# Seven block products for the u, gate_c and xb projections of the mixer, with the convolution's taps on ScalarE and GpSimd

## The reference

```python
z = h @ w_in                                   # h is rmsnorm(x, mix_norm)
za, zb, zg = jnp.split(z, [2 * A_WIDTH, 2 * A_WIDTH + 3 * B_WIDTH], axis=-1)
u, v = jnp.split(jax.nn.gelu(za), 2, axis=-1)
y_a = spatial_gating(u, v, sgu_norm, sgu_w, sgu_b) @ w_proj_a
gate_b, gate_c, xb = jnp.split(zb, 3, axis=-1)
y_b = (gate_b * short_conv(gate_c * xb, conv_w)) @ w_proj_b
g_a, g_b = jnp.split(zg, 2, axis=-1)
merged = jax.nn.sigmoid(g_a) * y_a + jax.nn.sigmoid(g_b) * y_b
return merged @ w_out
```

## Time and profile before

| | us |
|---|---|
| median of 3 runs | 1713.25 (1713.06 to 1713.26) |
| the profiled execution, whole | 1713.5 |
| its span in the trace | 1711.8 |
| TensorE busy (matmul) | 1690.5, 99% |
| VectorE, ScalarE, GpSimd busy | 947.4, 736.7, 758.2 |
| the twelve units that change | 953.2 to 1083.9 |
| the gate_b units behind them | 1083.9 to 1134.7 |

### The profile page before, as it was taken

One profiled execution on the slowest core, in us unless ns is written; L12 is line 12 of the kernel. 1 busy time (PEld: TensorE's weight loads), 2 busy tenths in 40 slices (PEclk: granted clock), 3 DMA queues, 4 the chain that ended last, 5 costly groups with the idle time before them and its releaser, 6 DMA issues.

```text
span 1711.8 us, 25456 instructions
## 1 busy us (share of the span) xinstructions
PE 1690.5 (99%) x9725; PEld 1445.4 (84%) x9725; DVE 947.4 (55%) x1313; ACT 736.7 (43%) x1027; POOL 758.2 (44%) x366
## 2 busy tenths in 40 slices
PE   7999999999999999999999999999999999999998
PEld 4677788777788899998889888888888889999887
DVE  4645765665766777877220634641112587777412
ACT  4444773644573544445333322332222454445323
POOL 1342635233225454555444544344444445554552
PEclk9999999999999999999999999999999999999999
DMA  9614215112112223322323222222222222232222
GB/s 362 240 52 171 75 50 221 50 74 99 50 50 98 99 99 111 110 90 85 102 101 114 102 94 98 99 85 92 96 95 99 99 99 99 98 114 83 97 89 83
DMA packets 35061, 180.88 MB, mean 106 GB/s; under 512 B 4486, under 2 KB 6668, under 8 KB 19372
## 3 DMA queue, kind: packets, MB, share of 16 engines
q1 hardware_dynamic: 30876, 166.09, 27.1%
q10 hardware_dynamic: 4112, 13.80, 2.1%
HBM read 177.78 MB, written 2.10 MB: 105 GB/s over the span
## 4 chain that ended last, share of the span: by engine, by line
PE 89%; issue 4%; POOL 3%; SPq 1%; DVE 1%; DMA 1%; ACT 1%; POOLq 0%; DVEq 0%; ACTq 0%
PE ps L1354 22%; PE ps L1356 21%; PE ps L1355 21%; PE ps L1656 4%; PE ps L1658 3%; PE ps L1657 3%; POOL wl_both L659 3%; PE ps L1416 2%; PE ps L1421 2%; PE ps L1417 2%; PE ps L1723 1%; PE ps L1697 1%; SPq L566 1%; DMA ada_w<-w_ada 1%; PE ps L1710 1%
## 5 line engine op out<-in xcount | busy, mean ns | idle before, releaser
L659 POOL TENSOR_TENSOR wl_both<-raw_both,wh_both 128x1024 fp32r<-128x1024 f32 (+1 forms) x184 | 425.2, 2331 | 509.8 <-ACT wh_both L794 505.7
L1354 PE MATMUL ps<-xh,wh_both 128*128 128x512 f32 (+1 forms) x880 | 315.2, 358 | 1.2 <-POOL wl_both L681 1.2
L1356 PE MATMUL ps<-xh,wl_both 128*128 128x512 f32 (+1 forms) x880 | 312.1, 355 | 0.0
L1355 PE MATMUL ps<-xl,wh_both 128*128 128x512 f32 (+1 forms) x880 | 312.0, 355 | 0.0
L794 ACT ACTIVATE wh_both<-raw_both 128x2048 fp32r<-128x2048 f32 x91 | 174.2, 1915 | 317.4 <-PE ps L1356 306.0
L681 POOL TENSOR_TENSOR wl_both<-raw_both,wh_both 128x1024 fp32r<-128x1024 f32 x46 | 114.2, 2498 | 206.8 <-ACT wh_both L948 137.9
L1354 PEld LDWEIGHTS ps<-xh,wh_both 128*128 128x128 f32 x880 | 166.4, 189 | 31.5 <-issue 7.5
L1356 PEld LDWEIGHTS ps<-xh,wl_both 128*128 128x128 f32 x880 | 166.4, 189 | 23.6
L1355 PEld LDWEIGHTS ps<-xl,wh_both 128*128 128x128 f32 x880 | 166.5, 189 | 22.3
L703 POOL TENSOR_TENSOR wl_both<-raw_both,wh_both 128x1024 fp32r<-128x1024 f32 x72 | 131.9, 1854 | 105.7 <-DVE ps L2593 105.7
L1354 PE MATMUL ps<-fh,wh_both 128*128 128x512 f32 (+1 forms) x374 | 141.4, 378 | 1.0 <-issue 1.0
(11 more groups left out here) (362 smaller groups left out, 3990.2 us busy)
## 6 DMA issues: line engine op xcount, KB each, us to landing
raw_both<-ffn_in_stream SPq DMA_DIRECT2D x44, 1024.0 KB, 4.8
raw_both<-mixer_stream SPq DMA_DIRECT2D x40, 1024.0 KB, 4.8
raw_both<-layer_stream SPq DMA_DIRECT2D x36, 1024.0 KB, 5.9
raw_both<-ffn_out_stream SPq DMA_DIRECT2D x32, 704.0 KB, 4.1
ada_w<-w_ada SPq DMA_DIRECT2D x16, 512.0 KB, 11.3
ada_late<-w_ada ACTq DMA_DIRECT2D x16, 512.0 KB, 4.9
gate_w<-w_ada ACTq DMA_DIRECT2D x4, 1024.0 KB, 13.2
next_w<-w_ada SPq DMA_DIRECT2D x7, 512.0 KB, 8.9
```

The costliest lines, as they stand in the source:

```text
L659: last = nc.gpsimd.tensor_tensor(wl[u][:, cols], raw[u][:, cols], wh[u][:, cols].bitcast(F32), ALU.subtract)
L1354: nc.tensor.matmul(bank_ap, w0, x0, start=first, stop=False, skip_group_check=goes_on)
L1355: nc.tensor.matmul(bank_ap, w0, x1, start=False, stop=False, skip_group_check=goes_on)
L1356: return nc.tensor.matmul(bank_ap, w1, x0, start=False, stop=last, skip_group_check=goes_on)
```

## The change

Twelve units of the mixer (4 of u, called units 0 to 3 below, and 8 of gate_c and xb, units 4 to 11) are made by seven block products each. The normalised input is kept once more, as `xs2`, and four combinations of its quarters are made during the v units. The spatial gate's scaling of v, its squares included, goes from VectorE to ScalarE. Of the convolution, the product gate_c x xb and the additions go to GpSimd, and the scaling by the taps' weights to ScalarE. The loads of `ws_t` and `bs` are issued after unit 10, since their place holds weight sums until then. The sum over the taps is finished on GpSimd (`taps`), one unit late; behind unit 11 the product, the taps and then the split of the first gate_b chunk follow on GpSimd in this order.

TensorE:

```diff
-            first_feature_unit(unit, chunk, (xh, xl), SPLIT0["norm3b"])
-            feature_unit(0, unit, chunk, 1, both_x)
-            with pe.Fori(1, (M_U + M_CX) // 2) as i:
+            def seven(i, c, u, first=False):
+                n_ = SEVEN + c + u
+                b = 2 * u + 1
...
+                    pe.wait_ge(seven_act, i * 6 + (3 * n_ - 1))
+                half_ready(i, chunk + c, u, 0)
+                block(0, True, blocks((wh, wl), 1), tokens(QT, 0)).then_inc(seven_mm, 1)
...
+                pe.wait_ge(s_low, i * 2 + (n_ + 1))
+                block(b, True, blocks((mea_h, mea_l), 0), mt2).then_inc(seven_mm, 1)
...
+                    pe.wait_ge(seven_dve, i * 8 + 4 * n_)
+                block(2, True, blocks((wh, wl), 3), mt1).then_inc(seven_mm, 1)
...
+                pe.wait_ge(seven_act, i * 6 + (3 * n_ + 1))
+                block(0, False, blocks((wh, wl), 0), tokens(0, 0)).then_inc(seven_mm, 1)
+                pe.wait_ge(seven_dve, i * 8 + (4 * n_ + 1))
+                block(b, False, blocks((mea_h, mea_l), 1), mt3).then_inc(seven_mm, 1)
+                pe.wait_ge(seven_dve, i * 8 + (4 * n_ + 2))
+                block(2, False, blocks((mea_h, mea_l), 2), tokens(0, 1)).then_inc(seven_mm, 1)
+                pe.wait_ge(seven_dve, i * 8 + (4 * n_ + 3))
+                half_ready(i, chunk + c, u, 1)
+                block(b, False, blocks((wh, wl), 2), mt4).then_inc(tile_done, 2)
```

GpSimd:

```diff
+            def padded_product(c):
+                u, j = c % 2, c - M_U
+                pool.wait_ge(banks_free[u], UNIT0["mixer"] + M_V + c - u + 4)
+                pool.wait_ge(seven_act, 3 * (SEVEN + c) + 2)
...
+                nc.gpsimd.memset(tpad[:, u, S + 1:S + 2], 0.0)
+                nc.gpsimd.tensor_tensor(tpad[:, u, 1:S + 1], act_u[:, u], act_g[:, u], ALU.mult).then_inc(m_prod, 1)
+
+            def taps(c):
+                u, j = c % 2, c - M_U
+                pool.wait_ge(seven_act, 3 * (SEVEN + c) + 3)
+                for c0, piece in enumerate(tap_piece):
+                    at_ = slice(2 + c0 * HALF, 2 + c0 * HALF + HALF)
+                    last = nc.gpsimd.tensor_tensor(tpad[:, u, at_], tpad[:, u, at_], piece[:], ALU.add)
+                last.then_inc(cv_ready, 1)
+                pool.wait_ge(cv_ready, 2 * j + 1)
+                nc.gpsimd.tensor_tensor(cv[:, j], cv[:, j], tpad[:, u, 2:S + 2], ALU.add).then_inc(cv_ready, 1)
...
+                    split_three(0, M_V, plain, 0, None)
+                    for c in range(MIXED):
+                        if c > M_U:
+                            padded_product(c - 1)
+                        if c < MIXED - 1:
+                            split_three(0, M_V + c + 1 - (c + 1) % 2, plain, (c + 1) % 2, None)
+                        if c > M_U:
+                            taps(c - 1)
+                    padded_product(MIXED - 1)
+                    taps(MIXED - 1)
+                    with pool.Fori((M_V + MIXED) // 2, count // 2) as i:
+                        for u in range(2):
+                            split(size, i, chunk, plain, u)
```

ScalarE:

```diff
+            def tap_first(c):
+                j = c - M_U
+                act.wait_ge(m_prod, j + 1)
...
+                nc.scalar.activation(cv[:, j], tpad[:, c % 2, 0:S], ACT.Copy, scale=conv2_w[:, j, 0:1])
+                for c0, piece in enumerate(tap_piece):
+                    last = nc.scalar.activation(piece[:], tpad[:, c % 2, 1 + c0 * HALF:1 + c0 * HALF + HALF], ACT.Copy,
+                                                scale=conv2_w[:, j, 1:2])
+                last.then_inc(m_tap, 1)
+                act.wait_ge(m_tap, j + 1)
+                nc.scalar.activation(tpad[:, c % 2, 2:S + 2], tpad[:, c % 2, 2:S + 2], ACT.Copy,
+                                     scale=conv2_w[:, j, 2:3]).then_inc(seven_act, 1)
+
+            for c in range(MIXED):
+                u, n_ = c % 2, SEVEN + c
+                if c < MIXED - 1:
+                    blocks_high(c + 1)
+                if c > M_U:
+                    tap_first(c - 1)
+                act.wait_ge(banks_free[u], unit + c - u + 2)
+                act.wait_ge(seven_mm, 6 * n_ + 1)
+                nc.scalar.activation(kept_m1[:, u], ps[:, 0, 0:HALF], ACT.Copy).then_inc(seven_act, 1)
+                if c < MIXED - 1:
+                    sums_high(c + 1)
+                act.wait_ge(seven_mm, 6 * n_ + 4)
+                if c < M_U:
+                    nc.scalar.activation(u2[:, 2 * c, 0:HALF], ps[:, 0, 0:HALF], ACT.Gelu_apprx_tanh
+                                         ).then_inc(seven_act, 1)
+                    act.wait_ge(banks_free[u], unit + c - u + 4)
...
+                    nc.scalar.activation(u2[:, 2 * c, HALF:S], u2[:, 2 * c, HALF:S], ACT.Gelu_apprx_tanh)
+                    nc.scalar.activation(u2[:, 2 * c + 1], u2[:, 2 * c + 1], ACT.Gelu_apprx_tanh
+                                         ).then_inc(seven_act, 1)
+                    nc.scalar.activation(v2_sq[:], v2[:, c], ACT.Square, accum_out=ss_v[:, 0, c:c + 1]
+                                         ).then_inc(m_root, 1)
...
+            act.wait_ge(tile_done, 2 * (unit + MIXED - 1))
             act.dma_start(ws_t[:], ins["sgu_w_t"]).then_inc(sgu_in, 16)
             act.dma_start(bs[:].rearrange("p h q -> p (h q)"), ins["sgu_b"].to_broadcast([P, KT * P])
                           ).then_inc(sgu_in, 16)
+            take_high(chunk + MIXED)
+            tap_first(MIXED - 1)
```

VectorE (`up_first` of the unit before first, then the next unit's sums with `keep_u2` between them, as in the feed-forward):

```diff
+            def sums(c, between=None):
...
+                nc.vector.tensor_tensor(ps[:, 4], a21, a22, ALU.add).then_inc(s_sums, 1)
+                nc.vector.tensor_tensor(ps[:, 6], a11, a21, ALU.subtract)
+                if between is not None:
+                    keep_u2(between)
...
+                if c:
+                    up_first(c - 1)
+                if c < MIXED - 1:
+                    sums(c + 1, c)
+                    two_lows(c + 1)
...
+                nc.vector.tensor_tensor(kept_m15[:], ps[:, 2, 0:HALF], kept_m1[:, u], ALU.add).then_inc(seven_dve, 1)
...
-                link(nc.vector.tensor_tensor(tpad[:, u, 1:S + 1], ps[:, 2 * u + 1], gc[:, u], ALU.mult))
-                dve.sem_inc(banks_free[u], 2)
-                dve.sem_inc(m_prod, 1)
-                link(nc.vector.tensor_scalar(cv[:, j], tpad[:, u, 0:S], conv2_w[:, j, 0:1], None, ALU.mult))
-                for tap in (1, 2):
-                    link(nc.vector.scalar_tensor_tensor(out=cv[:, j], in0=tpad[:, u, tap:tap + S],
```

More of the change, by code:

```diff
@@ L73 @@
 SEVEN = FT - STD
+MIXED = M_U + M_CX
+SEVENS = SEVEN + MIXED
+LATE_FIRST = (4, 5, 6, 7, 0, 1, 2, 3)
 QT = KT // 2
@@ L608, in _ @@
                     runs = ((0, 4), (4, count))
+                elif n == 4:
+                    runs = ((0, M_V + 2), (M_V + 2, M_V + MIXED + 2), (M_V + MIXED + 2, count))
                 else:
@@ L741, in _ @@
                     with pool.Fori(1, count // 2) as i:
+                        for u in range(2):
+                            split(size, i, chunk, plain, u)
+                    plain += count
+                    continue
+                if n == 4:
+                    with pool.Fori(0, M_V // 2) as i:
+                        for u in range(2):
+                            split(size, i, chunk, plain, u)
+                    split_three(0, M_V, plain, 0, None)
[9 more added lines that the diff above has]
+                    with pool.Fori((M_V + MIXED) // 2, count // 2) as i:
                         for u in range(2):
@@ L1441, in first_token_unit @@
                 chunk_ready(0, chunk - u, u)
-                for k in range(KT):
+                ks = range(KT) if low0 is not None else LATE_FIRST
+                for k in ks:
                     if sums_of is not None and k == KT // 2:
@@ L2059, in _, with block @@
             chunk += M_V
-            first_feature_unit(unit, chunk, (xh, xl), SPLIT0["norm3b"])
-            feature_unit(0, unit, chunk, 1, both_x)
-            with pe.Fori(1, (M_U + M_CX) // 2) as i:
+            def block(bank, first, weights, moving):
+                for j in range(QT):
+                    cols = slice(j * P, j * P + P)
+                    last = products(ps[:, bank, 0:HALF], (weights[0][:, cols], weights[1][:, cols]),
+                                    (moving[0][:, j], moving[1][:, j]), first and j == 0, j == QT - 1,
+                                    goes_on=not first)
+                return last
@@ L2063, in _ @@
+            seven(0, 0, 0, first=True)
+            seven(0, 0, 1)
+            with pe.Fori(0, (MIXED - 2) // 2) as i:
                 for u in range(2):
-                    feature_unit(i, unit, chunk, u, both_x)
+                    seven(i, 2, u)
+            pe.wait_ge(seven_act, 3 * (SEVEN + MIXED) - 1)
             unit += M_U + M_CX
@@ L2766, in _ @@
+            up_first(MIXED - 1)
+            unit += MIXED
+            dve.wait_ge(m_prod, M_CX)
             dve.wait_ge(sgu_in, 32)
```

297 lines of the change are left out of this document (215 added, 82 removed).

## The result

The changed kernel took 1732.35 us (median of 4, 1732.13 to 1734.24) beside 1713.26 for the kernel before (median of 4, 1713.06 to 1714.3): ratio 1.0113, 95% interval 1.0095 to 1.013, so 19.1 us slower. The forecast was 1738.6 with a range of 1725 to 1748. The profiled execution took 1732.3, its span 1730.4, which is 18.6 more than before.

What follows compares the result with a forecast made beforehand. TensorE, busy 99% of the span, was taken to bound the kernel. -9.6 + 0.4 + 3.6 + 1.4 + 16.3 + 1.6 + 9.0 = +22.7, plus 2.7 for the clock, +25.4 on 1713.25: 1738.6 us, range 1725 to 1748.

Steps and rivals of the forecast that it cites:

- The gain: Twelve mixer units at 10.08 us instead of 10.88 by seven products: -9.6 us, all on TensorE's path.
- The edge of a unit: A unit whose fourth product waits for `keep_m1` loses another 0.6 us at the sixth, by a fixed 3.44 us stretch.
- Units 0 to 4: Late Gelus and square on ScalarE delay the fourth product: units 1 to 4 at 10.97 us, +3.6; unit 0 +0.4.
- Units 5 to 11: Loop through GpSimd, ScalarE, VectorE, 13.3 us a unit: +16.3 for units 6 to 10, unit 5 +1.4, unit 11 +1.6.
- the port's term: In the loop, two VectorE sums hold up GpSimd's last tap and next product: 2 x 0.5 us.
- Rival (a): Loop with port free and short GpSimd instructions: 12.0 us a unit, 1726.5 to 1729 with the clock; chance 0.14.
- The seam: Gate_b's first chunk waits behind unit 11's product, taps and split on GpSimd: 9.0 us lost, bounds 8 to 10.5.
- The preparation in the v units: xs2, combinations, parts and first sums add about 13 us to VectorE, 4 to ScalarE, hidden: nothing lost.
- The clock: Granted clock falls during the seam and is low when gate_b begins: 2.7 us, middle of nothing and 5.4.
- (b): Hand-overs cost 0.05 to 0.1 more each than in the feed-forward: +28 to +31, 1742 to 1750; chance 0.16.
- (c): TensorE's fourth product is not stopped; units give 9.6, the seam takes 9.0: 1712.7 to 1713.5; chance 0.08.
- (d): Loop of the gate_c and xb units at 10.5 to 11 us: about 1718 to 1723; chance 0.06.

Runs made afterwards that it cites:

- all_three: The edits of loop_late, gelu_late and seam_first together, against the changed kernel: 1704.94 us, ratio 0.9949 to the kernel before.
- gelu_late: Changed kernel with a u unit's late Gelus and square moved behind ScalarE's keeping of the next unit's first product: 1729.64 us.
- loop_late: Changed kernel with ScalarE keeping the first product before it does the taps' scaling, instead of after: 1718.38 us.
- product_twice: Changed kernel with GpSimd multiplying gate_c and xb twice, the second time over the first result: 1747.55 us.
- filler_short: Changed kernel with 32 unused constant products on TensorE between the first gate block and the first gate_b tile: 1731.04 us.
- seam_first: Changed kernel with GpSimd splitting the first gate_b chunk before the last product and its taps: 1723.08 us.
- no_port: Changed kernel with VectorE's first two weight sums reading one input from PSUM instead of SBUF, so the sums themselves are left out: 1730.53 us.

## Why the prediction was right, and where it was off

**The gain** of 9.6 was real: all_three has 8.5 of it in the same stretch, with units of 10.0 to 10.14 but one of 10.48 that waits 0.21 at the sixth product.

**The edge of a unit.** Right: a unit that waits at the fourth product loses about 0.6 more at the sixth (2.01 - 1.44 = 0.57).

**Units 0 to 4.** Right in the sum, 10.91 against 10.97, and off inside it. The fourth product began 978.26 - 973.86 = 4.40 after the edge, not 4.65, so 0.1 late and not 0.3. Then the fourth and the sixth product, each behind a wait, take 1.53 instead of 1.44, for their second matmul comes 0.23 after the first and not 0.12; I had this 0.1 only inside the stretch from the fourth to the sixth. That is 0.08 + 0.09 + 0.57 + 0.09 = 0.83 a unit. The end of ScalarE's chain in unit 2, the square and `kept_m`:

```profile
975.43 1.04 ACT L1410 ACTIVATE v_sq<-v 128x1024 f32<-128x1024 f32 x1
...
977.85 0.36 ACT L1398 ACTIVATE kept_m<-ps 128x256 f32<-128x256 f32 x1
```

It ends 4.35 after the edge where I had 4.5: the terms add up to 4.83, and in this trace each of the five joints between ScalarE's instructions overlaps by 0.1. Unit 0 lost nothing (10.13) where I had 0.4. gelu_late confirms the cause.

**Units 5 to 11.** The mechanism was right: loop_late takes it away and product_twice lengthens it. The step that was off is the port's term, "another 2 x 0.5": it is once 0.4. I had both sums delay GpSimd, but only the first does; the second waits for the product itself. The stage of memset and product was 1.81 for 2.35, which is 2.7 over five units; the cheaper additions in three of the five are another 1.3. The rest of the 4.2 is small: the split took 3.60 for 3.65, and 13.3 - 10.08 is 3.22, where I had 3.25. Rival (a) took the additions as cheap and the port as free: a part of each is true, and the time lies between its 1729 and my 1738.6. The waits in the trace are accordingly up to 1.74 at the fourth product, not 2.7.

**The seam.** 8.6 against 9.0, with the same releaser, GpSimd's split. `bs` did come late, by 0.62 ("up to 1 us"). The preparation in the v units, put at nothing, cost nothing: unit 0 began 0.4 earlier than before.

**The clock.** The forecast was 2.7 as the middle of 0 to 5.4; the trace has 1.7, because the matmuls were slow for only 3.6 us of the tile (below). The 2.7 was the middle between two bounds and not worked out, so that it came near is luck. That it fell at the seam was right, and filler_short shows the cause.

**Rivals (b), (c), (d).** No hand-over was dearer than in the feed-forward: the stretch with most of them, 2.36, was forecast at 2.35. So (b) did not come. And the fourth product was stopped from unit 1 on. all_three shows that (c)'s units exist, with another order of the program; (c) as it stood, with this order, did not come. Nor did (d): the loop was at 12.3 to 12.7, not at 10.5 to 11.

**Sums in the prediction that do not come out.** By its own terms the loop's bounds are 11.7 (12.3, less 0.16 for the additions and 0.48 for the copies) and 13.8 (13.3 + 0.3 + 0.2), not 11.5 and 14.1; rival (a)'s five units at 12.0 are 9.6, not 9.8. Nothing of the forecast rests on them.

## What to carry to other kernels

Engines at 45% to 57% can together set the pace: follow one product's way through all engines until it comes back to where it began, add that up, and compare it with the bound engine's unit. If it is longer, first look for an instruction in the loop that needs nothing from the one ahead of it on its engine; moving `kept_m` ahead gave 14 us here without taking any work away. At a border between stages, let the engine that others wait for make what the next stage needs before it finishes the last one.

## What the runs showed of the hardware

**The clock can fall inside a unit, and the length of the wait before it doesn't decide it.** Windows of PE after: length, busy us (instructions) of PE, PEld, DVE, ACT, POOL, granted clock, DMA share, GB/s.

```profile
1036.00:1038.00 2.00, 1.34 (x7) 1.34 (x8) 1.27 (x3) 0.61 (x2) 0.00 (x0) 0.74 0.00 0
1038.00:1040.00 2.00, 2.00 (x12) 2.00 (x10) 1.34 (x3) 1.51 (x2) 1.40 (x1) 0.50 0.00 0
1040.00:1042.00 2.00, 2.00 (x17) 2.00 (x17) 1.41 (x4) 1.74 (x3) 2.00 (x2) 0.91 0.00 0
...
1060.00:1064.00 4.00, 2.26 (x20) 2.25 (x20) 1.73 (x3) 2.08 (x5) 0.31 (x1) 1.00 0.00 0
...
1096.00:1100.00 4.00, 0.00 (x0) 0.00 (x0) 0.00 (x0) 2.81 (x3) 3.35 (x4) 0.80 0.00 0
1100.00:1104.00 4.00, 2.32 (x6) 1.86 (x7) 0.00 (x0) 0.00 (x0) 4.00 (x3) 0.50 0.00 0
```

Behind the wait of 1.74 at 1036.66 the clock fell to 1.2 GHz (0.50), though TensorE was at work again; behind the wait of 1.74 at 1061.75 it did not fall. In seam_first, whose units up to there have the same lengths, it was the other way round (1.00 in 1036 to 1042, 0.72 in 1061 to 1065). I had counted on a fall only at the seam. Unit 7 took 13.50 by it, but the next one 11.59: the loop went round in 12.39 there, 0.1 more than the 12.27 of the same buffer elsewhere, so the slow matmuls were paid out of time in which TensorE would have waited. What decides whether it falls is open.

**What a slow clock costs.** PE's timeline after, in the first gate_b tile:

```profile
1103.13 0.63 PE L1488 MATMUL ps<-xh,wh_both 128*128 128x512 f32 x1
1103.55 0.63 PE L1489 MATMUL ps<-xl,wh_both 128*128 128x512 f32 x1
...
1105.26 0.39 PE L1490 MATMUL ps<-xh,wl_both 128*128 128x512 f32 x1
1105.48 0.39 PE L1488 MATMUL ps<-xh,wh_both 128*128 128x512 f32 x1
```

Matmuls of 512 columns follow each other at 0.42 to 0.43 and then, from 1105.26, at 0.22 to 0.23. From 1101.68 to 1105.26 are 3.6 us at half speed, of which half is the loss, 1.7 to 1.8. By the Trainium skill (TensorE: Matmul & The Clock Gate, Part 1) the clock comes back only after sustained work; the trace agrees: TensorE was at work from 1101.68, and the matmuls were slow until 1105.26.

**GpSimd's additions of the same form have two durations.** 1.45 and 1.31 in one unit, 1.23 and 1.09 in the next, in turn with the buffer of `tpad`, with the port's waits and without (in no_port 1.45 and 1.30, then 1.22 and 1.10). Why was not tried; it stays open.
